# First norm of a two-block float32 network: the scale chunks of the modulation computed by TensorE, with the opening order of the weight stream changed

## The reference, cut to what matters

```python
c_act = jax.nn.silu(c)
mod = c_act @ w_ada[l] + b_ada[l]            # 1024 -> 9 * 1024
sh1, sc1, g1, sh2, sc2, g2, sh3, sc3, g3 = jnp.split(mod, N_MOD, axis=-1)
x = x + 0.5 * g1 * swiglu(modulate(x, sh1, sc1), ffn1_gate[l], ffn1_up[l], ffn1_down[l])
# modulate(x, shift, scale) = rms_norm(x) * (1 + scale) + shift
# swiglu(u, wg, wu, wd)     = (silu(u @ wg) * (u @ wu)) @ wd
```

## Time and profile before

| | us |
|---|---|
| median of 3 runs (2253.9 to 2261.05) | 2259.08 |
| span of the profiled execution | 2258.5 |
| own time of the profiled execution | none is recorded beside the span; the span lies inside the runs, 0.6 below their median |
| PE busy / DVE busy / ACT busy | 2177.8 / 1526.8 / 1182.8 |
| PE's share of the chain that ended last | 81% |

### The profile page before, as it was taken

One profiled execution on the slowest core, in us unless ns is written; L12 is line 12 of the kernel. 1 busy time (PEld: TensorE's weight loads), 2 busy tenths in 40 slices (PEclk: granted clock), 3 DMA queues, 4 the chain that ended last, 5 costly groups with the idle time before them and its releaser, 6 DMA issues.

```text
span 2258.5 us, 40704 instructions
## 1 busy us (share of the span) xinstructions
PE 2177.8 (96%) x16754; PEld 1932.4 (86%) x16754; DVE 1526.8 (68%) x2122; ACT 1182.8 (52%) x2059; POOL 369.9 (16%) x360
## 2 busy tenths in 40 slices
PE   7999999999999999999999999999999988999998
PEld 7888988988888889988888988788878978868887
DVE  6897767688778866767775874387557544626753
ACT  4554557565455544765554664365446431526542
POOL 0111022111102100311111103020232350303001
PEclk9999999999999999999999999999998999999999
DMA  7887662467768768434665443355524300434552
GB/s 277 328 308 252 242 244 94 149 236 259 243 232 295 274 214 315 161 103 165 214 223 186 166 159 130 131 170 186 177 91 150 103 4 12 160 129 146 190 186 95
DMA packets 114232, 417.79 MB, mean 185 GB/s; under 512 B 12672, under 2 KB 12928, under 8 KB 113664
## 3 DMA queue, kind: packets, MB, share of 16 engines
q1 hardware_dynamic: 113184, 410.34, 52.2%
q10 hardware_dynamic: 864, 4.84, 0.6%
HBM read 414.09 MB, written 1.05 MB: 184 GB/s over the span
## 4 chain that ended last, share of the span: by engine, by line
PE 81%; DVE 7%; ACT 5%; issue 4%; POOL 1%; DMA 1%; POOLq 0%; SPq 0%; DVEq 0%; ACTq 0%
PE banks L551 80%; DVE weight_lower L1520 1%; DVE weight_ring L1531 1%; POOL heap L2718 1%; ACT weight_upper L2230 1%; ACT xn_t L2354 1%; PE banks L954 1%; PE banks L1340 0%; DMA weight_ring<-w_ada_dram 0%; ACT L2264 0%; ACT xn_t L2277 0%; DMA weight_ring<-w_in_dram 0%; ACT heap L2387 0%; DMA weight_ring<-ffn_up_dram 0%; ACT xn_halves L2245 0%
## 5 line engine op out<-in xcount | busy, mean ns | idle before, releaser
L551 PE MATMUL banks<-xn_halves,weight_upper 128*128 128x512 f32 (+1 forms) x3680 | 1004.8, 344 | 11.3 <-DVE weight_lower L1520 8.1
L1520 DVE TENSOR_TENSOR weight_lower<-weight_ring,weight_upper 128x1024 fp32r<-128x1024 f32 x580 | 743.1, 1287 | 315.4 <-ACT weight_upper L2230 314.2
L551 PE MATMUL banks<-xn_halves,weight_lower 128*128 128x256 f32 x2832 | 802.0, 283 | 6.6 <-DVE xn_halves L1553 2.9
L2230 ACT ACTIVATE weight_upper<-weight_ring 128x1024 fp32r<-128x1024 f32 x580 | 607.9, 1054 | 351.7 <-PE banks L551 202.6
L551 PEld LDWEIGHTS banks<-xn_halves,weight_upper 128*128 128x128 f32 x3680 | 637.6, 190 | 99.5 <-issue 7.9
L551 PEld LDWEIGHTS banks<-xn_halves,weight_lower 128*128 128x128 f32 x2832 | 538.6, 190 | 9.9 <-DVE xn_halves L1553 3.2
L551 PE MATMUL banks<-hidden,weight_upper 128*128 128x512 f32 x1216 | 430.0, 397 | 0.0
L551 PE MATMUL banks<-hidden,weight_lower 128*128 128x256 f32 x1216 | 341.7, 281 | 0.0
L551 PEld LDWEIGHTS banks<-hidden,weight_upper 128*128 128x128 f32 x1216 | 228.6, 188 | 56.4
L2718 POOL TENSOR_TENSOR heap<-heap 128x256 f32<-128x256 f32 x120 | 122.0, 1021 | 930.5 <-ACT heap L2460 614.5
L551 PEld LDWEIGHTS banks<-hidden,weight_lower 128*128 128x128 f32 x1216 | 228.2, 188 | 0.0
(11 more groups left out here) (299 smaller groups left out, 2496.1 us busy)
## 6 DMA issues: line engine op xcount, KB each, us to landing
weight_ring<-w_ada_dram SPq DMA_DIRECT2D x144, 512.0 KB, 4.5
weight_ring<-ffn_gate_dram SPq DMA_DIRECT2D x88, 512.0 KB, 3.8
weight_ring<-ffn_up_dram SPq DMA_DIRECT2D x88, 512.0 KB, 4.5
weight_ring<-ffn_down_dram SPq DMA_DIRECT2D x88, 512.0 KB, 3.4
weight_ring<-m_w_up_dram SPq DMA_DIRECT2D x64, 512.0 KB, 3.2
weight_ring<-m_w_down_dram SPq DMA_DIRECT2D x64, 512.0 KB, 3.2
weight_ring<-w_in_dram SPq DMA_DIRECT2D x58, 512.0 KB, 4.0
weight_ring<-b_w_rkv_dram SPq DMA_DIRECT2D x24, 512.0 KB, 3.2
```

The source lines that it names most:

```text
L551: return nc.tensor.matmul(o, w, r, start=first, stop=last)
L1520: V.tensor_tensor(w_lo[:, n % RING, :], ring[:, n % RING, :], w_hi[:, j % SPLITS, :].bitcast(F32), ALU.subtract).then_inc(*did("weight_low ...
L2230: A.activation(w_hi[:, j % SPLITS, :], ring[:, n % RING, :], ACT.Copy).then_inc(*did("weight_upper", j))
```

## The change

The scale segment of layer 0 is no longer summed by DVE from 8 ada chunks. A new input `w_scale` has the same numbers as matmul tiles, 8 whole chunks; PE sums each with 8 float32 matmuls with one moving column, silu(c) as a column (`scale_sums`), into one column of bank 3 or 6, and DVE adds the bias (`scale_mod`). ACT computes silu of that column, and `vecs`, in which it lies, is loaded ahead of `c_rows`.

PE's program begins with 24 matmuls of 128 columns on a tile of ones, then the squares, `scale_sums` 0 and 1, the spread (the 4 matmuls of hold ahead of it and the 60 behind it are gone), `scale_sums` 2 to 6, 16 matmuls of hold, the waits for the first three cuts, `scale_sums` 7, 8 matmuls of hold, and the three products. The stream is: scale 0, ada 0, scale 1, ada 1, ..., ada 5, scale 6 (13 chunks), three cuts, ada 6, scale 7, ada 7, then the rest. ACT makes the first three upper halves ahead of tile 5's shift, DVE the lower halves ahead of ada 6; ACT works ahead in general only after the whole shift. The 32 ada chunks of the first SwiGLU come one a step for f = 6 to 21 and two in each of the 8 down steps.

```diff
-        ADA_FIRST = [seg * KD + k for k in range(KD) for seg in (1, 0)]
+        ADA_FROM, CUTS_FROM = 6, 6
@@ sync
+            sp.dma_start(vecs[:, :], dram["vecs"]).then_inc(*did("vecs_in", 0, by=16))
             sp.dma_start(c_rows[:, :], dram["c_rows"]).then_inc(*did("c_in", 0, by=16))
-            sp.dma_start(vecs[:, :], dram["vecs"]).then_inc(*did("vecs_in", 0, by=16))
@@ ada_step
                     chunks = [seg * KD + k for seg in ADA_AT[s] for k in range(KD)]
+                    if s == 0:
+                        up, each = KF - ADA_FROM, 2
+                        at = step - ADA_FROM if step < KF else up + each * (step - KF)
+                        if step >= ADA_FROM:
+                            ada_take(chunks[at:at + (1 if step < KF else each)])
+                        return
@@ spread
-                hold(7, 4)
+                hold(7, 4 if n else 0)
...
-                if n != "mem":
-                    hold(7, 8 if n else 60)
+                if n not in (0, "mem"):
+                    hold(7, 8)
+            def scale_sums(k):
+
+                b = 3 if k % 2 else 6
+                refill(b)
+                w, used = arrived("w_scale", k)
+                for j in range(KD):
+                    mn = mm(bank[:, b, k:k + 1], w[:, j * P:(j + 1) * P], vec("c", j), j == 0, j == KD - 1)
+                mn.then_inc(*did("scale_raw", k, also=[used]))
+                readers[b] = [("scale_mod", k)]
@@ project_wide_first
+                first = len(order)
                 took = [(*cut(name, i), done, readers_of, b) for name, i, done, readers_of, b in items]
-                ada_take(after)
+                if after:
+                    slot_of["cuts"] = first + len(items)
+                    after()
+            def last_scales():
+
+                for k in range(CUTS_FROM, KD):
+                    ada_take([k])
+                    if k + 1 < KD:
+                        scale_sums(k + 1)
+                hold(7, 8)
+
             def ffn(s, l, which, norm, next_norm):
                 spread(norm)
+                if s == 0:
+                    for k in range(2, CUTS_FROM + 1):
+                        scale_sums(k)
+                        if k < CUTS_FROM:
+                            ada_take([k])
+                    hold(7, 16)
...
                 project_wide_first(items(0) + items(1)[0:1], xn_hl, ("normed_lower", norm),
-                                   ADA_FIRST[KD + 4:] if s == 0 else ())
-                if s == 0:
-                    hold(7, 8)
-                else:
-                    ada_step(s, 0)
+                                   last_scales if s == 0 else None)
+                ada_step(s, 0)
                 for f in range(1, KF):
-                    if s or f > 3:
-                        ada_step(s, f)
-                    elif f == 3:
-                        for step in range(f + 1):
-                            ada_step(s, step)
+                    ada_step(s, f)
@@ start of the tensor program
+            pe.wait_ge(*of("warm", 0))
+            for _ in range(24):
+                mm(cols(7, P), silu[:, 0, 0:P], silu[:, 0, 0:P], True, True)
             pe.wait_ge(*of("consts_in", 0))
             for k in range(KD):
                 squares_sum(0, k, KD)
-            ada_take(ADA_FIRST[:KD + 4])
+            pe.wait_ge(*of("c_col", 0))
+            for k in range(2):
+                scale_sums(k)
+                ada_take([k])
@@ vector
+            def scale_mod(k):
+
+                dve.wait_ge(*of("scale_raw", k))
+                V.tensor_tensor(mod[:, KD + k:KD + k + 1], bank[:, 3 if k % 2 else 6, k:k + 1], vec("b_ada", KD + k),
+                                ALU.add).then_inc(*did("scale_mod", k))
+                dve.wait_ge(*of("scale_mod", k))
@@ normalise
-                        modulated(KD + k, k)
+                        modulated(k)
+                        if k > 1:
+                            scale_mod(k)
@@ start of the vector program
             bias_steps()
-            modulated(KD, 0, KD + 1, 1, KD + 2, 2)
+            dve.wait_ge(*due("bias_half", 0))
+            modulated(0)
+            scale_mod(0)
             rstd(0)
-            modulated(KD + 3, 3)
+            modulated(1)
+            scale_mod(1)
@@ scalar, shift
-                    if k == KD - 2:
-                        starting[0] = False
+                    if n == 0 and k == CUTS_FROM - 1:
+                        work_ahead(slot_of["cuts"])
@@ scalar, start
+            act.wait_ge(*due("vecs_in", 0))
+            A.activation(vec("c", 0, KD), vec("c", 0, KD), ACT.Silu).then_inc(*did("c_col", 0))
             act.wait_ge(*due("c_in", 0))
@@ gpsimd
+            G.memset(silu[:, 0, 0:P], 1.0).then_inc(*did("warm", 0))
```

More of the change, by code:

```diff
@@ L122 @@
             ("b_in", 2 * KD), ("gate_b", 2 * KD), ("lam", KD), ("b_out", KD), ("mu", 6 * KD),
-            ("w0", KD), ("a0", KD), ("k_k", KD), ("k_a", KD), ("r_k", KD), ("gn_g", KD), ("gn_b", KD)]
+            ("w0", KD), ("a0", KD), ("k_k", KD), ("k_a", KD), ("r_k", KD), ("gn_g", KD), ("gn_b", KD), ("c", KD)]
 VEC_AT, VEC_W = packed(VEC_COLS)
@@ L672, in project_wide, with project_wide_first @@
                 readers[b] = readers_of
-            def project_wide_first(items, x, ready, after=()):
+            def scale_sums(k):
[6 more added lines that the diff above has]
+                readers[b] = [("scale_mod", k)]
+            def project_wide_first(items, x, ready, after=None):
                 for *_, b in items:
                     refill(b)
+                first = len(order)
                 took = [(*cut(name, i), done, readers_of, b) for name, i, done, readers_of, b in items]
-                ada_take(after)
+                if after:
+                    slot_of["cuts"] = first + len(items)
+                    after()
                 for k in range(KD):
@@ L1525, in work_ahead @@
                         half = 0.5 if i // KD % NMOD in (2, 8) else 1.0
-                        if n == 0:
+                        if i == 0:
                             dve.wait_ge(*of("c_act", 0))
@@ L2430, in _ @@
                     shift(n, lambda k: mods(l, 3 * s3, k))
+                    starting[0] = False
                     if s3 == 1:
@@ L2841, in laid_out @@
              "a_b_out_2", "b_mu_2", "b_w0_2", "b_a0_2", "b_k_k_2", "b_k_a_2", "b_r_k_2",
-             "b_gn_g_2", "b_gn_b_2"))], 1)
+             "b_gn_g_2", "b_gn_b_2", "c"))], 1)
     d["w2"] = np.concatenate([np.stack([a[n][l] for l in L for n in ("cmpk_w2", "cmpv_w2")], 1)] * 2, 0)
@@ L2845, in laid_out @@
     d["w_ada"] = each(lambda l: a["w_ada"][l].T.reshape(-1, P, D))
+    d["w_scale"] = tiles(a["w_ada"][0][:, D:2 * D])
     d["c_rows"] = np.repeat(a["c"], P, 0)
```

## The result

The changed kernel took 2267.18 us in the median of 20 runs (2260.23 to 2274.46), beside 2260.84 us of the kernel before in 20 runs on the same chip (2253.9 to 2266.43): a ratio of 1.0021, 95% interval 1.0011 to 1.003 (the two medians divided give 1.0028; the ratios here and below come, with their intervals, from the single runs). Both allow a cost of some 2.5 to 5 us, which is under 0.3%. Forecast were 2260 us and no difference, with a range of 2247 to 2266. The median by itself lies 1.2 us above that range; but the range was laid on a median of 2259.08 us for the kernel before, which in 20 runs is 1.8 us higher.

What follows compares the result with a forecast made beforehand. PE was taken as the bound, through when its unbroken run of products starts: group end 56.5 plus 0.3 us stall, less the old 55.5, gave +1.3 us on 2259.1, so 2260 us, with a range of 2247 to 2266.

Steps and rivals of the forecast that it cites:

- `c_rows` and the squares: Opening: `c_rows` lands at 8.14 us, squares start at 9.5 and take PE 3.7 us at the fast pace.
- The narrow sums' clock: Opening: scale sums 0 to 6 run at the slow pace, 1.2 GHz, taking 24.4 us against 12.9 at the fast one.
- fast sums: Rival, opening: the clock stays at 2.4 GHz through the narrow sums, 11.5 us less, total 2247.6 us; chance 20%.
- Hold of 16: Opening, behind scale sums 2 to 6: 32 instructions take 5.7 us, with the clock rising inside; ends 3.6 and 7.0.
- Scale sum 7: Opening, behind the hold of 16 matmuls: one scale sum at the fast pace, 1.8 us.
- Hold of 8: Opening, between scale sum 7 and the first three products: 1.8 us.
- rises late: Rival, opening: the clock rises only after the hold of 16, adding 4.7 us, total 2265 us; chance 9%.
- The group's end: First SwiGLU: the products of the first three cuts end at 56.5 us.
- Up 2: Behind the first group: this weight chunk, issued as the group ends, stalls PE 0.3 us, 1.3 at most.
- The down steps: First SwiGLU's down steps, 16 ada chunks instead of 8 or 9: cost 0, with 8 us as upper end.
- The rival: Down steps: two sums a step make PE wait in each of 8 steps, total 2268 us; chance 8%.
- The mark: 55.5 us, where the old first group would have ended without stalls or slow clock behind it; the new start must beat it.

Runs made afterwards that it cites:

- e1: The changed kernel run again with no edit: 2264.29 us, ratio 1.0007 to the kernel before.
- e2: The changed kernel with the scale sums' one moving column repeated to 128 columns: 2257.11 us, ratio 0.9969 to the kernel before.
- f3: The changed kernel with 128 moving columns for the scale sums and for the first norm's squares: 2253.04 us, ratio 0.9958 to the kernel before.
- e4: The changed kernel with the old order of the 32 ada chunks: 2269.29 us, ratio 1.0022 to the kernel before.
- f2: The changed kernel with the attention constants loaded at step 2 instead of 8: 2266.62 us, ratio 1.0024 to the kernel before.
- g1: The kernel before run again with no edit, for its trace: ratio 1.0008 to the kernel before.
- e3: The kernel before with only the new order of the 32 ada chunks: 2259.49 us, ratio 0.9985 to the kernel before.
- f1: The changed kernel with 1 opening matmul instead of 24: 2275.67 us, ratio 1.0061 to the kernel before.
- g2: The changed kernel with 1 opening matmul instead of 24, run once more: 2275.11 us, ratio 1.0063 to the kernel before.

## Why the prediction was right

Right was the mechanism: the gain on DVE is paid by PE in slow narrow sums, and the two nearly balance. By its steps, with the first trace of the changed kernel and e1's behind it:

- *`c_rows` and the squares.* Landing forecast at 8.14 us, it was 8.06; squares forecast from 9.5, they came at 9.57 and 9.54. They took 3.70 in e1, as forecast, and 5.33 in the first trace, where the clock fell within them; the sum had no bounds for that.
- *The narrow sums' clock*, on which all hung: sums 0 and 1 in 6.96 and 6.41 us (7.0), sums 2 to 6 in 17.07 both times (17.5), the spread 1.20 (1.19). e2 shows the rival "fast sums" for what it is: true if the clock is held, which narrow sums don't do. Its group end was 43.2 and e2's 45.21. Of these 2.0 us, 0.9 are e2's first sums, still partly slow (f3 ends at 44.26); the rest goes with PE's waits for `w_scale` chunks, which f3 has as well. Its price of 11.5 us was too high by the times (5.6 under the kernel before). In the trace e2 ends the first SwiGLU 7.4 us earlier than before (223.44 for 230.87), while it runs its gate and up steps from 37 to 170 us at the slower of two paces (below), worth 2.5; with the 2.0 of the group end that makes 11.9, close to the 11.5, but the 2 us by which the times fall short of the trace aren't placed.
- *Hold of 16*: 6.67 and 5.60 (5.7, bounds 3.6 to 7.0). Scale sum 7: 1.84 twice (1.8). Hold of 8: 2.03 (1.8). The rise comes inside the hold, so the rival "rises late" is out, but by little: in the six traces with narrow sums the hold takes 5.60 to 6.67, and 7.0 was where that rival began. By these lengths the rise comes an estimated 4.1 to 6.3 us behind the narrow sums. The sum took 4.5 from the work resumed at 266.77 us, but there the clock fell only at 268.1 and was back at 271.5, so the row is another case, and that its value served is partly luck.
- *The group's end*: 57.41 and 54.27 (56.5), with 55.88 and 55.97 in e4 and f2. A forecast to 1 us was partly luck, as the same opening varies by 3.1.
- *Up 2*: no wait at all (0.3 forecast). But a wait of 0.8 us near 110 us was missed. The warning stood in the trace of before: there too a gate chunk, issued at 97.13 us beside the constants' load of 97.15, kept ACT waiting, and landed after 8.2 us, just in time. Nothing in the sum asked which other queue issues a load beside a weight chunk. ACT's wait for it, in the kernel before and then in the changed one:
```profile
105.31 1.06 ACT L2230 ACTIVATE weight_upper<-weight_ring 128x1024 fp32r<-128x1024 f32 x1 [5.60 <-DMA weight_ring<-ffn_gate_dram]
```
```profile
109.12 1.06 ACT L2274 ACTIVATE weight_upper<-weight_ring 128x1024 fp32r<-128x1024 f32 x1 [6.85 <-DMA weight_ring<-ffn_gate_dram]
```
- *The down steps*: 0 forecast; PE waits for nothing there, with two ada chunks a step. The rival is out, though with little to spare: in f2 the last 15 us of the chain go by DVE's and ACT's work on these steps.
- *The mark*, 55.5 us for the old start, and the sum of +1.3 us. Against it the starts of the last wide product give +4.8 and +2.5 (+6.0 and +3.8 against g1's trace). e4 checks the old stalls' worth: its last 960 instructions of the SwiGLU start at 69.98 us (chain 171.01 us), those of before at 62.00 (169.40). So with the old order kept, the new opening costs 8.0 us, not the 9.8 by which its group ends later (55.88 for 46.11).

One term was not in the sum at all, a second pace of the wide products. From 80 to 100 us and from 140 to 160, before and then e1:
```profile
80.00:100.00 20.00, 20.00 (x117) 17.62 (x117) 17.88 (x24) 11.93 (x19) 2.96 (x4) 1.00 0.78 268
...
140.00:160.00 20.00, 20.00 (x117) 17.62 (x116) 18.27 (x24) 12.45 (x20) 3.21 (x4) 1.00 0.80 279
```
```profile
80.00:100.00 20.00, 20.00 (x115) 17.34 (x114) 17.07 (x22) 11.94 (x19) 2.97 (x4) 1.00 0.76 261
...
140.00:160.00 20.00, 20.00 (x115) 17.38 (x114) 18.10 (x22) 10.72 (x16) 2.23 (x3) 1.00 0.83 289
```
The clock reads 1.00 in all four and PE is busy throughout, yet 117 instructions go by in one kernel and 115 in the other. A pair of products starts every 0.3466 us or every 0.3534 in the mean. Over the gate and up steps that is 1.2 us in the first trace, which goes slow at 113 us, and 2.4 us in e1. Less that, the two traces give +3.6 and +0.1 for the change, with the forecast's +1.3 between them; the wait near 110 (0.8 and 0.7 us) is in both. By the mark it would be 57.41 and 54.27, less 55.5, and the wait: +2.7 and -0.5, so 0.9 and 0.6 us are left that no term has. Part of the agreement is luck, then: the sum is within 2.5 us for each trace, and what it left out is as large as its result. The pace isn't of the change: other stages of either kernel show both (below).

The Trainium skill's advice in "TensorE: Matmul & The Clock Gate", "Why this matters for your kernels", to keep TensorE busy, was weighed against the rows of before and the rows were followed. The trace disagrees with that advice for narrow sums: PE was busy for all of the 20 us from 20 to 40, and its clock was 0.50. The measurement decides.

## What to carry to other kernels

Moving small sums from DVE to PE relieves DVE, but here a long stream of one-column matmuls ran at half of PE's clock, and the wide work behind it started slow as well. Repeating the moving column to 128 with a broadcast cost nothing per instruction (0.114 us for 0.115 at the same clock) and held the clock (7.31 us for 64 instructions instead of 13.6). When a change has parts, measure each alone: here one cost about 5 us and the other gained about 3, and only the sum looked like no change.

## What was not expected of the hardware

- *Two paces at one granted clock.* The chain's lines of the same work differ by 1.3%, before and then e1:
```profile
453.96 186.79 PE banks L551 x1056
```
```profile
456.33 184.46 PE banks L551 x1056
```
The kernel before again (g1) has 184.46 there as well. So it isn't a matter of the kernel. In the stages of wide products looked at, a pace holds for a whole stage and changes at the start of one or behind a wait. In the fourteen traces PE spent between some 500 us (g1) and some 1050 (e3) at the slower one, by a count of the pairs. At 2% that is an estimated 10 us between executions, more than the effect of the change. What decides it wasn't tried and is open.
- *Busy isn't enough.* PE at 10.00 of 10.00 us and at 1.2 GHz for more than 20 us, and 2.4 GHz when the same sums had 128 columns and PE was busy for 8.97.
- *A load beside a bigger one.* The 512 KB gate chunk issued 0.02 us before the constants' load took 9.40 us (9.44 in e1, 8.2 before); the median of such a load is 4.0.
- *The opening matmuls.* Without them f1 and g2 take 9 to 13 us more, for 0.5 to 4.4 us that the traces show ahead of the first product. Why is open.
